# The first gathered tile's score search moves into the first steps of the dense part, its routing and its rows to later steps

## The reference, cut to what matters

```python
q = (x @ peer_wq).reshape(T, PEER_HEADS, 2, PEER_HALF)          # 8 heads, two halves
s = jnp.einsum('thpd,phkd->thpk', q, peer_keys)                 # 128 scores a half
sv, si = lax.top_k(s, 16)                                       # the search
cand = sv[:, :, 0, :, None] + sv[:, :, 1, None, :]
top_s, pos = lax.top_k(cand.reshape(T, 8, 256), 16)             # the routing
eidx = ...                                                      # 16 of 128*128 experts a head
gate = softmax(top_s)
act = gelu(einsum('cd,ced->ce', x, peer_u[eidx])) * gate        # 128 experts a token
out = einsum('ce,ced->cd', act, peer_v[eidx])
```

## Time and profile before

| | |
|---|---|
| median of three runs | 2613.67 us (2603.48, 2613.67, 2614.12) |
| profiled execution, own time | 2599.84 us |
| its span | 2598.0 us |
| PE busy | 2357.6 us, 91% |
| DVE busy | 1773.5 us, 68% |
| ACT busy | 493.8 us, 19% |
| POOL busy | 962.0 us, 37% |
| DMA | 647.01 MB, mean 249 GB/s |

### The profile page before, as it was taken

The page is one execution under the profiler, slowest core; times in us unless marked ns, Lnnn a source line. Parts: engine busy times, 40 slices in busy tenths (PEclk is TensorE's granted clock), DMA queues, the critical chain, the costliest instruction groups (busy, mean ns, idle before and its releaser), DMA issues.

```text
span 2598.0 us, 43625 instructions
## 1 busy us (share of the span) xinstructions
PE 2357.6 (91%) x18034; PEld 1660.0 (64%) x18034; DVE 1773.5 (68%) x3472; ACT 493.8 (19%) x994; POOL 962.0 (37%) x774
## 2 busy tenths in 40 slices
PE   6999969788888879997899799999999999998997
PEld 3555538577777764443488677776776677775664
DVE  2111362256677766675899886799899898875767
ACT  2111225234434421101112211000001000100101
POOL 0000000000355450543620005666665677774753
PEclk9999979889999988998999679999999999999998
DMA  8340130310566661867883028999999999999997
GB/s 323 141 167 37 64 122 3 122 42 14 176 225 205 208 223 41 320 243 257 324 315 123 18 70 319 368 395 381 408 406 353 409 409 405 388 401 412 409 409 305
DMA packets 163935, 647.01 MB, mean 249 GB/s; under 512 B 21062, under 2 KB 21958, under 8 KB 158298
## 3 DMA queue, kind: packets, MB, share of 16 engines
q0 software_dynamic: 110592, 402.70, 41.0%
q1 hardware_dynamic: 53146, 241.52, 24.0%
HBM read 635.50 MB, written 8.65 MB: 248 GB/s over the span
## 4 chain that ended last, share of the span: by engine, by line
PE 63%; DVE 15%; DMA 9%; issue 7%; ACT 4%; POOL 2%; another core or an unknown queue 1%; SPq 0%; DVEq 0%; POOLq 0%; ACTq 0%
PE ps L1094 9%; DMA arena<-in_peer_v,arena 8%; PE ps L1105 8%; PE ps L610 6%; PE ps L1116 5%; PE ps L1070 4%; PE ps L866 4%; DVE arena L2101 3%; PE ps L1010 2%; PE ps L977 2%; PE ps L1035 2%; POOL arena L2278 2%; PE ps L1020 2%; PE ps L614 2%; PE ps L834 1%
## 5 line engine op out<-in xcount | busy, mean ns | idle before, releaser
L1105 PE MATMUL ps<-arena 128*128 128x512 f32 x1024 | 465.6, 598 | 23.6 <-DVE arena L2140 23.3
L1094 PE MATMUL ps<-arena 128*128 128x256 f32 x2048 | 481.0, 389 | 0.0
L2278 POOL DMA_INDIRECT arena<-in_peer_u,arena x256 | 345.4, 1349 | 347.8 <-DVE arena L1894 193.0
L1094 PEld LDWEIGHTS ps<-arena 128*128 128x128 f32 x2048 | 392.9, 195 | 69.4 <-issue 19.6
L2278 POOL DMA_INDIRECT arena<-in_peer_v,arena x256 | 303.4, 1185 | 199.0 <-DVE arena L2101 131.9
L2101 DVE SCALAR_TENSOR_TENSOR arena<-arena 128x1024 f32<-128x1024 f32 x252 | 315.1, 1283 | 82.0 <-DMA arena<-in_peer_v,arena 75.3
L2266 POOL DMA_INDIRECT arena<-in_peer_u,arena x128 | 167.6, 1309 | 549.2 <-DVE arena L1894 317.7
L1105 PEld LDWEIGHTS ps<-arena 128*128 128x128 f32 x1024 | 194.3, 191 | 223.0 <-issue 208.7
L2096 DVE SCALAR_TENSOR_TENSOR arena<-arena 128x1024 bf16<-128x1024 f32 x256 | 303.0, 1221 | 31.1 <-DMA arena<-in_peer_u,arena 29.8
L1116 PEld LDWEIGHTS ps<-arena 128*128 128x128 bf16 x3072 | 206.3, 156 | 69.3 <-issue 47.2
L1116 PE MATMUL ps<-arena 128*128 128x32 bf16 x3072 | 209.2, 243 | 23.0 <-DVE arena L2133 22.4
(11 more groups left out here) (361 smaller groups left out, 3273.6 us busy)
## 6 DMA issues: line engine op xcount, KB each, us to landing
arena<-in_uT SPq DMA_DIRECT2D x128, 512.0 KB
arena<-in_peer_v SPq DMA_DIRECT2D x128, 512.0 KB
arena<-in_w_ada SPq DMA_DIRECT2D x12, 2048.0 KB, 21.7
arena<-in_peer_wq SPq DMA_DIRECT2D x12, 2048.0 KB, 9.5
arena<-in_w_in SPq DMA_DIRECT2D x6, 2048.0 KB, 7.5
arena<-in_w_out SPq DMA_DIRECT2D x4, 2048.0 KB, 7.6
arena<-in_peer_u,arena POOLq DMA_INDIRECT x384
arena<-in_peer_v,arena POOLq DMA_INDIRECT x384
```

Of the source, the lines that this page charges most:

```text
L1094: m = pe.matmul(ps[:, 4 + i % 2, 0:ND], us[i % UB][:, k, :], hTd[:, k, :], start=(k == 0), stop=(k == KD - 1))
L1105: m = pe.matmul(ps[:, 2 * r + c, :], sgel[:, i % SBUFS, P * r:P * r + P], vs[i % VB][:, 512 * c:512 * c + 512], start=(i == 0), stop=(i == ...
L2278: pool.indirect_dma_start(gring[:, n % RING, :], None, a[("peer_u", "peer_v")[e]][0], bass.IndirectOffsetOnAxis(ap=ids[:, t, m:m + 1], axi ...
```

## The change

It takes tile 1's search out of the loop over the 32 gate groups that stand ahead of step 0 and puts it into steps 0 to 3, four score rows each. Tile 1's routing goes from steps 0 to 5 (ten pieces a step) to steps 4 to 10 (nine a step), the end of it and route_sub from step 6 to 11, its gate_tile from step 7 to 12. `rows_by` counts from step 12 and not from step 7: 400 rows up to step 95 in both, so 400/83 and not 400/88 a step. From step 95 on it is as before. `FIRST_CALLS` is the count of search calls that must be done before peer_v's rows may be accumulated, since tile 2's scores lie in the accumulators; it is 4 + 8 for the new number of calls.

```diff
 def rows_by(i):
-    return max(0, min(EARLY, (i - 7) * EARLY // 88)) + max(0, min(ROWS - EARLY, (i - 95) * (ROWS - EARLY) // 31))
+    return max(0, min(EARLY, (i - 12) * EARLY // 83)) + max(0, min(ROWS - EARLY, (i - 95) * (ROWS - EARLY) // 31))
...
-FIRST_STEPS = {2: (24, 32)}
-FIRST_CALLS = EXPH + 8
-ROUTE_STEPS = {1: (0, 6), 2: (40, 54)}
+FIRST_STEPS = {1: (0, 4), 2: (24, 32)}
+FIRST_CALLS = 4 + 8
+ROUTE_STEPS = {1: (4, 11), 2: (40, 54)}
...
                 for g in range(d * GROUPS // 2, (d + 1) * GROUPS // 2):
                     one_hots(g)
-                    if g % 4 == 3:
-                        first_stage(1, g // 2 - 1, g // 2 + 1)
```

## The result

The changed kernel takes 2616.7 us (median of 20 runs, 2603.0 to 2632.9); the kernel before, measured beside it, 2606.8 us (20 runs, 2595.0 to 2615.9). The ratio is 1.004, with a 95% interval of 1.0023 to 1.0058: some 10 us slower, against 2 us faster as forecast. The time lies in the stated range, and the change is inside what I called "same", but it is clear of the measurement and has the other sign. The three runs shown ahead of the prediction (median 2613.67) also lay 7 us high.

The account below looks back on a forecast made before the run. Bound: queue bytes at 409.5 GB/s plus idle queue time once gathers run. Terms -18.3 + 49.1 - 14.9 - 17.9 = -2 us gave 2597.8 us for the profiled execution, median 2612; range 2597 to 2627.

Parts of the forecast that it names:

- same: Whole kernel: time within about 0.5%, 13 us, which a measurement can't tell from no change; chance 0.58.
- The bound: Once gathers run, the end is set by bytes at 409.5 GB/s plus the time the queues stand idle.
- Part 1: Gate groups ahead of step 0: moving the search out removes PE's waits, saving 18.3 us, bounds 10 and 23.
- Part 2: Steps 0 to 3: the search fits beside VectorE's other work, 7.6 us in PE's 8.45, and costs 0.
- Part 3: Routing in steps 4 to 11, rows from step 13: first row +49.1 us, minus 18.3, so 30.8 us later.
- the idle time of the queues: Stream of gathers: idle time falls from 35 to 17 us, a gain of 18, bounds 8 and 31.
- an emptier ring absorbs more: VectorE's full steps: an emptier ring of eight rows hides delay; idle 3 us in steps 24-31, 7.5 in 50-54.
- my own sum: Whole kernel: -18.3 + 49.1 - 14.9 - 17.9 = -2 us.
- VectorE leaves the queues idle: Slower rival: search and routing steps keep idle time at 35 us, +16 us, 2630; decides from 19 us; chance 0.18.
- the two signs of being wrong that I had named: Steps 56 to 90 at 8.44 us with PE never waiting, or queues below 380 GB/s over steps 24 to 54.
- PE's wait for `weigh`: Expected sign in the dense steps: this wait grows from step 30 on; no size given.
- after the low clock: hidden(2), behind the gate groups: takes 6.19 us just after the low clock, left so; possible gain 2 or 3 us.

Follow-up runs that it names:

- e3: Kernel before the change, v load of each dense step cut from 512 to 64 KB; ratio 0.9969 to the kernel before.
- e4: Changed kernel, v load of each dense step cut from 512 to 64 KB; ratio 0.9939 to the kernel before.
- e9: Changed kernel with e7's edits and the v load cut from 512 to 64 KB a step; ratio 0.9834 to the kernel before.
- old: The kernel before the change, measured beside the changed one; median 2606.8 us.
- e10: Kernel before the change, only tile 2's routing moved from steps 40-54 to 33-60; ratio 1.001 to the kernel before.
- e7: Changed kernel, tile 1's routing in steps 4-9, rows counted from step 9, tile 2's routing in steps 33-60; ratio 0.9950 to the kernel before.

## Why the prediction was wrong

- **The bound** was read rightly: queues at 409 to 411 GB/s in the tail, and e3, e4 and e9 show that relieving them speeds both orders up. The Trainium skill (DMA: Bandwidth & Descriptors, Specifications) gives 435 GB/s for the fabric and about 358 for HBM. The trace does reach 435, which I had overlooked when I wrote that no stretch has more than 410: it stands in the first microseconds of the kernel before, where SyncE's plain loads run alone.

```profile
8.00:28.00 20.00, 8.20 (x52) 2.54 (x56) 3.93 (x8) 7.99 (x14) 0.00 (x0) 0.98 1.02 435
```

Beside the gathers no run has more than 415 over 50 us, so 409.5 was the right number for this stretch; why the mix stays below the plain loads isn't shown. The 358 was passed in every stream with full loads (395 to 404).
- **Part 1** (18.3 us): 17.9 us by PE's groups (53.0 us for 70.9), and 1.3 more in hidden(2), 4.89 for 6.19.
- **Part 2** (nothing): right, no wait of PE in steps 0 to 12.
- **Part 3** (+49.1 - 18.3 = +30.8): +28.3. PE's lead at step 13 was 20.8 us and not 18.3: 19.1 at back(0), and nearly all of the rest between back(6) and back(7), which took 11.7 us before and 9.8 after; there the kernel before had a stretch of low granted clock (0.92 on the mean over 1564 to 1585). The bytes loaded meanwhile: -13.2 for -14.9.
- **The step that failed is the idle time of the queues**, "an emptier ring absorbs more": 17 us said, 28.8 measured. By place, forecast and measured: start 4 and 7.1 (POOL's first ten issues are 2.0 us apart, not 1.2); steps 24 to 31, 3 and 5.2; steps 50 to 54, 7.5 and 11.8, beyond my bound of 11; steps 40 to 49, 0 and 1.3; the rest 2.5 and 3.4. The ring is empty only where VectorE waits for landings. Ahead of the long pieces it doesn't: over steps 40 to 49 the changed kernel has one kind of wait on VectorE, and it isn't for a transfer, while POOL waits ten times for VectorE to free a slot.

```profile
DVE arena L2101 <- DVE arena L2101: 1.2, 2, 0.7
...
POOL arena L2276 <- DVE arena L2101: 18.1, 10, 3.1
```

I had found VectorE "level with the queues" there (8.8 against 8.7 us a step) and still counted on an empty ring behind it; over ten such steps it had filled. In steps 50 to 54 POOL then waits 19.4 us in four waits for VectorE to free a slot, and PE 10.1 us for `weigh`:

```profile
POOL arena L2276 <- DVE arena L2101: 19.4, 4, 10.2
```

```profile
PE ps L1105 <- DVE arena L2140: 10.1, 3, 7.0
```

- With 28.8 in place of 17 my own sum gives +10, and the terms had told me where the sign turns: at 19 us of idle time. I held the rival on the slow side ("VectorE leaves the queues idle") at 0.18. It is what happened, at somewhat over half its price: the idle time fell by 5 us, not by 0 and not by 18. A term that I could only bound between 8 and 31 (the bounds of its parts even add up to 9.5 and 32.5), with the sign turning at 19, left no ground for a forecast of either sign. Nor could the two signs of being wrong that I had named show it: steps 56 to 95 took 8.8 us each and the queues moved 383 GB/s over steps 24 to 54. Both watched the bound and not the size of the idle time. PE's wait for `weigh` doesn't grow from step 30 on either: it is 5.9 us in steps 24 to 31, none in 40 to 49, and 10.1 in 50 to 54.
- What I had counted as idle time of the queues alone is also an account of VectorE, which e4 shows and e9 bears out: over steps 24 to 55 the later start puts eight more rows on an engine that is full in most of them. While bytes are the bound it only keeps the idle time up; without them it costs some 8 us by itself (295.3 for 287.6).

Left open: how much of old's own 34 us of idle time can be won. e10 and e7 moved it about more than they removed it.

## What to carry to other kernels

When a long transfer runs beside a compute loop at its ceiling, an earlier loop moves the end only as far as the transfer starts earlier or stands idle less; ask when the transfer's first byte moves, and count the empty time ahead of it as lost, less what else is loaded in it. Here 19 us won ahead of the loop cost 28 us of later start because the table of steps, not the ids, held the rows back: the same search placement with the rows three steps sooner is 0.9% faster, one half by the start and one half by less idle time. A buffer hides a slow stretch only if it is empty when the stretch begins; whether it is stands in the consumer's waits just before, not in the mean rates.

## What the runs showed of the hardware that I had not expected

PE was granted half its clock (1.2 of 2.4 GHz) through nearly all of the gate groups even with no gap in them: 0.51 over 53 us in which it was busy 51.35, as 0.50 over 71 us with gaps. A group of 24 matmuls (128x32, bf16) took 1.63 us there (26.17 over 16 groups) and 1.52 us at the full clock in an early dense step (from 1519.01 to the next start at 1520.53), so for them the clock is worth 7%. For the fp32 matmuls it is worth more: hidden(2), the first behind them, took 4.89 us, and 6.19 before, against 3.69 for the one in the next step at the full clock. It didn't run after the low clock, as I had written, but partly in it: the granted clock was 0.50 in its first 5.1 us before and in its first 2.4 us after.
